# Adding the two halves of a compressed row by transfers and VectorE, and scoring all compressed keys of the prompt with the keys as the weights

## What is computed

```python
def compress(k, pe, wc):
    ...
    chunks = k[:, :n_chunk * CMP_STRIDE].reshape(bn, n_chunk, CMP_STRIDE, N_KV, HEAD_DIM)
    pe_r = pe.reshape(reps, CMP_STRIDE, 1, HEAD_DIM)
    w_r = wc.reshape(reps, CMP_STRIDE, HEAD_DIM, HEAD_DIM)
    return sum(jnp.einsum('bcsgh,she->bcge', chunks[:, r:r + n_cmp] + pe_r[r], w_r[r])
               for r in range(reps))

    # in the attention, for each query block
    s_c = jnp.einsum('bqgrh,bcgh->bqgrc', qg, kc) * scale
    p_c = masked_softmax(s_c, vis_c[None, :, None, None, :])
    o_c = jnp.einsum('bqgrc,bcgh->bqgrh', p_c.astype(vc.dtype), vc)
    ...
    o = g[..., 0:1] * o_c + g[..., 1:2] * o_s + g[..., 2:3] * o_w
```

## Time and profile before

| | |
|---|---|
| median of 3 runs | 821.28 us |
| the profiled execution | 820.7 us |
| its span in the trace | 819.1 us |
| TensorE matmul busy | 791.7 us (97%) |
| VectorE busy | 557.6 us (68%) |
| ScalarE busy | 392.7 us (48%) |
| mean granted TensorE clock | 0.993 |

### The profile page before, as it was taken

One profiled execution on the slowest core, in us unless ns is written; L12 is line 12 of the kernel. 1 busy time (PEld: TensorE's weight loads), 2 busy tenths in 40 slices (PEclk: granted clock), 3 DMA queues, 4 the chain that ended last, 5 costly groups with the idle time before them and its releaser, 6 DMA issues.

```text
span 819.1 us, 16906 instructions
## 1 busy us (share of the span) xinstructions
PE 791.7 (97%) x6364; PEld 731.9 (89%) x6364; DVE 557.6 (68%) x1044; ACT 392.7 (48%) x773; POOL 90.5 (11%) x165
## 2 busy tenths in 40 slices
PE   6999999999999999999789999999999999999994
PEld 6999598888889999999699987989888999999993
DVE  4676278887769675656567753698876886665664
ACT  4443236666365544443353422566655564444333
POOL 2330243000100000000023204410000000000000
PEclk9999999999999999999999999999999999999998
DMA  7877367542754655554357845665339456555531
GB/s 271 287 245 253 107 204 265 202 124 84 235 213 155 180 181 181 180 180 155 128 186 246 289 134 155 201 239 204 90 96 332 121 178 182 180 182 182 180 101 53
DMA packets 39482, 150.72 MB, mean 184 GB/s; under 512 B 5744, under 2 KB 5744, under 8 KB 38768
## 3 DMA queue, kind: packets, MB, share of 16 engines
q1 hardware_dynamic: 31104, 111.33, 42.0%
q0 software_dynamic: 8304, 38.37, 14.0%
HBM read 144.73 MB, written 13.34 MB: 193 GB/s over the span
## 4 chain that ended last, share of the span: by engine, by line
PE 92%; DVE 3%; ACT 3%; issue 1%; DMA 1%; SPq 0%; DVEq 0%; ACTq 0%
PE bank L594 22%; PE bank L595 22%; PE bank L596 22%; PE bank L678 3%; PE bank L798 3%; PE bank L628 1%; PE bank L642 1%; PE bank L748 1%; PE bank L605 1%; PE bank L754 1%; PE bank L839 1%; PE bank L919 1%; PE bank L680 1%; PE bank L778 1%; PE bank L728 1%
## 5 line engine op out<-in xcount | busy, mean ns | idle before, releaser
L594 PE MATMUL bank<-x_hi,w_hi 128*128 128x264 f32 x1200 | 351.6, 293 | 0.0
L596 PE MATMUL bank<-x_lo,w_hi 128*128 128x264 f32 x1200 | 341.1, 284 | 0.0
L595 PE MATMUL bank<-x_hi,w_lo 128*128 128x264 f32 x1200 | 340.8, 284 | 0.0
L1093 DVE TENSOR_TENSOR w_lo<-ring,w_hi 128x1024 fp32r<-128x1024 f32 x202 | 248.6, 1231 | 131.4 <-ACT w_hi L935 127.4
L935 ACT ACTIVATE w_hi<-ring 128x1024 fp32r<-128x1024 f32 x202 | 213.0, 1055 | 61.2 <-PE bank L596 34.3
L594 PEld LDWEIGHTS bank<-x_hi,w_hi 128*128 128x128 f32 x1200 | 226.8, 189 | 5.9 <-issue 4.9
L595 PEld LDWEIGHTS bank<-x_hi,w_lo 128*128 128x128 f32 x1200 | 227.0, 189 | 0.8
L596 PEld LDWEIGHTS bank<-x_lo,w_hi 128*128 128x128 f32 x1200 | 226.1, 188 | 0.0
L594 PE MATMUL bank<-h_rounded,w_hi 128*128 128x264 f32 x352 | 102.2, 290 | 0.0
L595 PE MATMUL bank<-h_rounded,w_lo 128*128 128x264 f32 x352 | 100.2, 285 | 0.0
L983 ACT ACTIVATE h<-bank 128x264 f32<-128x264 f32 x88 | 34.6, 393 | 121.2 <-PE bank L596 113.1
(11 more groups left out here) (239 smaller groups left out, 1002.6 us busy)
## 6 DMA issues: line engine op xcount, KB each, us to landing
ring<-weights_dram SPq DMA_DIRECT2D x206, 512.0 KB, 3.7
cache_a<-kcmp_dram POOLq DMA_DIRECT2D x32, 128.0 KB, 3.9
cache_b<-vcmp_dram POOLq DMA_DIRECT2D x32, 128.0 KB, 3.5
cache_a<-ksel_dram POOLq DMA_DIRECT2D x32, 128.0 KB, 2.7
cache_b<-vsel_dram POOLq DMA_DIRECT2D x32, 128.0 KB, 3.3
cache_a<-kwin_dram POOLq DMA_DIRECT2D x2, 2048.0 KB, 12.4
cache_b<-vwin_dram POOLq DMA_DIRECT2D x2, 2048.0 KB, 9.1
kv_dram<-h POOLq DMA_DIRECT2D x2, 1584.0 KB, 8.5
```

Of the source, the lines that this page charges most:

```text
L594: pe.matmul(out, w_high[:, k0 + k, :], high, start=(k == 0), stop=False)
L595: pe.matmul(out, w_rest[:, k0 + k, :], high, start=False, stop=False)
L596: ins = pe.matmul(out, w_high[:, k0 + k, :], rest, start=False, stop=(k == kn - 1))
L1093: dve.tensor_tensor(w_lo[:, slot % RING], ring[:, slot % RING], w_hi[:, d % HI_RING].bitcast(F32), ALU.subtract).then_inc(w_lo_ready, 1)
```

## The change

Three things are rewritten, and the order around them.

1. The halves of a compressed row are no longer added on TensorE. After the eviction SP copies each half of `halves` into the opposite partitions of a second buffer `other`, by two transfers of 64 x 640 elements for keys and two for values, on the queue of the weights. VectorE adds first half, second half and bias in one instruction for each of four blocks.
2. In `cmp_scores` the weights are now the 128 x 32 keys of `kc_bd`, four blocks of them beside each other in the array, and 256 query columns are the moving operand: 8 matmuls instead of 16. The scores come out transposed; ScalarE evicts them to `cs_t`, and a new step `cmp_back` turns them back by four transposes, from which VectorE goes on as before.
3. In the order, `cmp_vrows` moves behind `cmp_scores`, `cmp_soft` behind `dense 24`, and `cmp_turn` behind `dense 25`.

```diff
@@ -104,13 +104,11 @@
 order += [("cmp_k", 0), ("gates", 0), ("cmp_v", 0), ("cmp_sum", 0), ("cmp_sum", 1), ("dense", 21),
-          ("cmp_rope", 0), ("cmp_vrows", 0), ("dense", 22), ("cmp_scores", 0), ("dense", 23), ("cmp_soft", 0),
-          ("dense", 24)]
+          ("cmp_rope", 0), ("dense", 22), ("cmp_scores", 0), ("cmp_vrows", 0), ("dense", 23), ("cmp_back", 0),
+          ("dense", 24), ("cmp_soft", 0)]
     order.append(("scores", p))
-    if p == 0:
-        order.append(("cmp_turn", 0))
@@ -120,6 +118,8 @@
 nxt += 1
+if u == 0:
+    order.append(("cmp_turn", 0))
...
@@ -204,7 +202,7 @@
 "cmp_v": [OT, PT0], "cmp_rope": [MI],
-"cmp_vrows": [SB], "cmp_scores": [SA], "cmp_turn": [PT0], "one_cmp_scores": [SB],
+"cmp_vrows": [SB], "cmp_scores": [SA], "cmp_back": [PT1], "cmp_turn": [PT0], "one_cmp_scores": [SB],
@@ -249,8 +247,9 @@
 SPLIT_AT = plan_splits()
+CROSS_AFTER = {SLOT_CK: 0, SLOT_CV: 1}
 SLOTS_IN = [sum(1 for i in range(SLOTS) if i % RING == s) for s in range(RING)]
-VECTOR_STEPS = 101
+VECTOR_STEPS = 100
@@ -332,7 +331,9 @@
-halves = hf[:, 0:2 * 10 * 4 * CT].rearrange("p (v s g c) -> p v s g c", v=2, s=10, g=4)
+n_half = 2 * 10 * 4 * CT
+halves = hf[:, 0:n_half].rearrange("p (v s g c) -> p v s g c", v=2, s=10, g=4)
+other = hf[:, n_half:2 * n_half].rearrange("p (v s g c) -> p v s g c", v=2, s=10, g=4)
@@ -344,6 +345,7 @@
 cs = probs_flat[:, 768:768 + 32 * CT].rearrange("p (n c) -> p n c", c=CT)
+cs_t = probs_flat[:, 0:GP * SEQ]
...
@@ -438,6 +441,14 @@
+            def cross(l, which):
+
+                for j in range(2):
+                    wait_emptied(sp, l, ("cmp_k", "cmp_v")[which], 0, j)
+                for at in (0, HD):
+                    sp.dma_start(other[HD - at:2 * HD - at, which], halves[at:at + HD, which]
+                                 ).then_inc(other_landed[which], 16)
+
             load(slice(0, 1), 0)
@@ -454,6 +465,8 @@
 load(bass.ds(l * SLOTS + n, 1), i)
+if before in CROSS_AFTER and not following:
+    cross(l, CROSS_AFTER[before])
 if n == RING:
@@ -693,20 +706,9 @@
                         done(ins, step, i)
-                    elif step == "cmp_sum":
-
-                        out = out_bank(step, i)
-                        for j in range(2):
-                            wait_emptied(pe, l, "cmp_v" if i else "cmp_k", 0, j)
-                        for half in range(2):
-                            for g2 in range(2):
-                                ins = pe.matmul(out[g2 * HD:g2 * HD + HD, 0:10 * GP * NC].rearrange(
-                                    "p (s g c) -> p s g c", g=GP, c=NC), ident[:, half * HD:half * HD + HD],
-                                    halves[:, i, :, g2:4:2, half:half + NC], start=(half == 0), stop=(half == 1))
-                        done(ins, step, i)
                     elif step == "cmp_rope":
                         out = out_bank(step, i)
-                        wait_emptied(pe, l, "cmp_sum", 0)
+                        pe.wait_ge(kc_summed, l + 1)
                         done(pe.matmul(out[:, 0:288], perm, kc_all[:, :, :, :].rearrange("p g s c -> p (g s c)"),
@@ -722,12 +724,20 @@
     pe.wait_ge(roped, (l + 1) * len(ROPED))
+    for gp in range(GP):
+        for r in range(R):
+            ins = pe.matmul(out[32 * r:32 * r + 32, gp * SEQ:(gp + 1) * SEQ],
+                            kc_bd[:, gp, :, :].rearrange("p a b -> p (a b)"),
+                            h[:, Q + gp * R + r, 0:SEQ], start=(gp == 0), stop=(gp == GP - 1),
+                            skip_group_check=True)
+    done(ins, step, i)
+elif step == "cmp_back":
+    out = out_bank(step, i)
+    wait_emptied(pe, l, "cmp_scores", 0)
     for qi in range(2):
-        for n in range(8):
-            col = qi * 256 + n * 32
-            ins = pe.matmul(out[:, col:col + 32], h[:, Q + n, (1 - qi) * P:(2 - qi) * P],
-                            kc_bd[:, n // R, :, :].rearrange("p a b -> p (a b)"),
-                            start=True, stop=True)
+        for gp in range(GP):
+            col, src = qi * 256 + gp * P, gp * SEQ + (1 - qi) * P
+            ins = pe.transpose(out[:, col:col + P], cs_t[:, src:src + P], ident)
@@ -995,6 +1005,9 @@
         "p s g c -> p (s g c)"), bank[FILL[step, i, 1][0]][:, 0:CMP_OWN // KT8], ACT.Copy), step, i, 1)
+elif step == "cmp_scores":
+    wait_filled(act, l, step, i)
+    emptied_by(act.activation(cs_t, bank[SA][:, :], ACT.Copy), step, i)
@@ -1211,19 +1224,27 @@
 elif step == "cmp_sum":
-    which = i
-    b = FILL[step, i, 0][0]
-    wait_filled(dve, l, step, i)
-    link(dve.tensor_copy(bias[:, which:which + 1], bank[b][:, 18 * NC:18 * NC + 1]))
-    out = (vc_all if which else kc_all)[:, :, :, 0:NC].rearrange("p g s c -> p s g c")
-    src = bank[b][:, 0:18 * NC].rearrange("p (s g c) -> p s g c", g=GP, c=NC)
-    for gp in range(GP):
-        ins = dve.tensor_scalar(out[:, :, gp, :], src[:, :, gp, :], bias[:, which:which + 1], None,
-                                ALU.add)
-        if gp == 0:
-            link(ins)
-    emptied_by(ins, step, i)
-    if which:
+    dve.wait_ge(other_landed[i], (l + 1) * 2 * 16)
+    all_of = vc_all if i else kc_all
+    for g2 in range(2):
+        rows = slice(g2 * HD, g2 * HD + HD)
+        first, second = (other, halves) if g2 else (halves, other)
+        ins = dve.tensor_tensor(bias[rows, i:i + 1], first[rows, i, NB + 1, g2, 0:1],
+                                second[rows, i, NB + 1, g2, 1:2], ALU.add)
+    link(ins)
+    for g2 in range(2):
+        rows = slice(g2 * HD, g2 * HD + HD)
+        first, second = (other, halves) if g2 else (halves, other)
+        for gp in range(GP):
+            ins = dve.scalar_tensor_tensor(
+                out=all_of[rows, gp, 0:NB + 1, 0:NC], in0=first[rows, i, 0:NB + 1, 2 * gp + g2, 0:NC],
+                scalar=bias[rows, i:i + 1], in1=second[rows, i, 0:NB + 1, 2 * gp + g2, 1:CT],
+                op0=ALU.add, op1=ALU.add)
+    if i == 0:
+        ins.then_inc(kc_summed, 1)
+        dve.wait_ge(kc_summed, l + 1)
+    else:
+        link(ins)
@@ -1251,12 +1272,12 @@
                                bank[SB][:, 2 * P:4 * P]), step, i)
-elif step == "cmp_scores":
+elif step == "cmp_back":
     for qi in range(2):
-        ins = dve.tensor_tensor(cs[:, qi * 16:qi * 16 + 16, :], bank[SA][:, qi * 256:qi * 256 + 256]
+        ins = dve.tensor_tensor(cs[:, qi * 16:qi * 16 + 16, :], bank[PT1][:, qi * 256:qi * 256 + 256]
```

More of the change, by code:

```diff
@@ L196, in banks_of @@
         return [(PT0, PT1)[i]]
-    if step == "cmp_sum":
-        return [(PT1, SA)[i]]
     if step == "one_scores":
@@ L388, in trunk @@
         cmp_in_ready = sem("cmp_in_ready")
+        other_landed = [sem("other_k_halves_landed"), sem("other_v_halves_landed")]
         v_new_ready = sem("v_new_ready")
@@ L391, in trunk @@
         cmp_out_ready = sem("cmp_out_ready")
-        kc_ready = sem("kc_ready")
+        kc_ready, kc_summed = sem("kc_ready"), sem("kc_summed")
         cmp_shifted, cmp_exped, cmp_probs = sem("cmp_shifted"), sem("cmp_exped"), sem("cmp_probs")
```

## The result

The changed kernel is slower. Its median is 831.7 us (830.59 to 832.25, 4 runs), that of the kernel before, on the same chip, 821.71 us (820.14 to 822.3, 4 runs): 10 us more, a ratio of 1.0121 with a 95% interval of 1.0106 to 1.0136. The forecast was 822.0 us and its range ended at 825.6, so the measured time lies outside both. The profiled execution of the changed kernel took 832.25 us with a span of 830.6, against 820.7 and 819.1.

What follows compares the result with a forecast made beforehand. TensorE, busy 97% of the span, was taken as the bound. Its 4.44 us saving per layer met two waits: layer 1 +1.3, layer 2 -0.3, so 820.7 + 1.0 = 821.7, predicted as 822.0 us; range 818.6 to 825.6.

Steps and rivals of the forecast that it cites:

- TensorE issues 4.44 us less in a layer: TensorE's own work: 5.73 us of sums and scores gone, 1.29 of new scores and `cmp_back` added, in each layer.
- The values' transfers land at 104.6: First wait, layer 1: transfers issued about 100.9, queued behind the weight load, at the stores' pace, 0.3 us for page loads.
- the late bound of 105.8: Late end of the values' landing: 328 KB at the weight load's pace take 2.4 us after that load lands at 103.4.
- 103.0: Early end of the values' landing, from stores landing 2.1 us after issue; the early-landing rival had chance 0.10.
- VectorE needs 4.7 us from there to the keys: VectorE after the landing: sums, `vc_rep`, a weight's rest, rotation with `kc_bd`; keys ready at 109.3, TensorE waits 3.3 us.
- From the keys to `scores 0` 7.7 us, with the clock left at full: TensorE from 109.3 to 117.0: scores 0.9, `cmp_vrows` 0.39, a product 3.0, `cmp_back` 0.39, a product 3.0.
- The 1.5 us of layer 2, "taken as gone": Layer 2's loss at half clock behind the old compressed scores, 1.5 us, assumed to vanish with the change.
- The softmax chain is 2.4 us longer: Second wait: from `scores 0` to the second `turn` 17.66 us instead of 15.25, the compressed exponential coming behind `dense 24`'s eviction.
- the forecast's 134.7: Layer 1's restart in the second `turn`: 117.0 + 17.66, against 133.41 before, +1.3 us.
- The rival "values land late or the clock falls": Slower rival at TensorE's wait for `kc_ready`: late landing +1.2 in each layer, each clock fall +1.5; 824.4 to 828.5, chance 0.27.
- "A wait of 5 us (then 825 and more)": Sign that the forecast is wrong: TensorE waiting 5 us ahead of the compressed scores, where 2.5 to 4 was expected.
- a landing after 105.3 or one fall: Threshold for the slower rival: values landing after 105.3 in both layers, or one fall of the clock.

Runs made afterwards that it cites:

- the fillers: The changed kernel plus 48 extra matmuls with unused results, put right ahead of TensorE's wait for `kc_bd`; 826.47 us, ratio 1.0064.

## Why the prediction was wrong

Point by point, in layer 1, by its own steps:

- *TensorE issues 4.44 us less in a layer.* Right: it reached the wait at 106.01 (forecast 106.0), and with full clock the eight scores took 1.0 us (0.9).
- *The values' transfers land at 104.6.* **This step failed.** They were there at 107.1, 2.5 us later and beyond the late bound of 105.8. Two terms were mis-sized. GpSimd's pages, taken at 0.3 us by choice, cost 1.8 in these rows (some 1.3 by the means). And the pace was taken from four stores to DRAM: with the pages away it was still 4.73 us from first issue to use (4.35 in layer 2), where the forecast, without its 0.3 for the pages, had 3.7 (from 100.6, the first of its two issues, to 104.3). The issue, too, was taken at 0.33 us and takes 0.55. Each bound rested on one kind of transfer, and neither counted the other queue. In layer 2 it is 5.65 us from issue to use. The rule of the Trainium skill (DMA: Bandwidth & Descriptors, "Two DMAs through the same engine are not ordered") that was read as speaking against 103.0 pointed the right way: with the transfers in front of the load it was 2.3 us less from issue to use in layer 1, and 1.1 in layer 2.
- *VectorE needs 4.7 us from there to the keys.* 5.07 (107.12 to 112.19). The four sums took 1.27 us as four overlapping instructions (1.0), and the two tiny ones 0.32.
- *From the keys to `scores 0` 7.7 us, with the clock left at full.* **This step failed too**: 10.11, and 9.76 in layer 2. With the fillers it was 7.85 and 7.87, so 2.3 and 1.9 us are the clock's. The clock had a place among the rivals, at 1.5 us a fall; it fell in both layers, and for 6.8 us, where the stretch around had lasted 3.4. The 1.5 us of layer 2, "taken as gone", went the wrong way as well. That an idle TensorE loses its clock is also a rule of the Trainium skill (TensorE: Matmul & The Clock Gate, "Part 1: The HAM clock gate"); the run with the fillers agrees, with 2.3 us in layer 1. It isn't the only thing that goes before a fall here: the one at 513.9 in the kernel before came behind no wait.
- *The softmax chain is 2.4 us longer.* Right: 2.25 (17.50 against 15.25), with 1.86 at `scores 1` (forecast 1.8) and 1.22 at the second `turn` (1.5).

Layer 1: 2.5 + 0.4 + 2.4 - 0.2 = 5.1 us over the forecast's 134.7, which makes the 139.80. Layer 2: stage A is 4.2 us over the forecast (18.65 - 14.4), of which the longer wait (5.33 us against 3.3) has 2.0 and the clock most of the rest; the chain is as forecast (2.4 longer), and TensorE reaches `cmp_rope` 0.4 us earlier than forecast: 3.8. The fall at the last layer norm, which the runs tie to no part of the change, adds 1.7. Together 10.6 on 821.7 gives 832.3, against the profiled 832.25.

The rival "values land late or the clock falls" was what happened, with its place and mechanism as written; but its two parts were priced as mishaps that meet now and then (0.27, at most 828.5), where the first brought the second each time: in the four profiled kernels in which TensorE waited, with nothing to fill the time, 4.0 to 6.2 us behind the values, the clock fell in both layers. How long it stayed down did not follow the wait: 6.8 us in seven of the eight layers, and 3.4 behind 4.06 us in the eighth, while 4.04 us were followed by 6.8. "A wait of 5 us (then 825 and more)" was the sentence that fitted. The range was too narrow because its late end left out most of what the pages take of the DMA engines, and let the clock fall once. Its threshold was loose as well: a landing after 105.3 or one fall gives 823.1 or 823.2 by the forecast's own prices, not yet the 823.7 that it called slower.

## What to carry to other kernels

Work taken off the bounding engine pays only if nothing it waits for stands behind the new path: here the same instructions gave 831.7 or 814.98 us by the place of two steps in the order, so put the step that waits for a transfer behind the one the bounding engine needs, before judging the transfer. Bound the landing of a new transfer by everything that is on the DMA engines in that window, the loads of the same queue and those of other queues, not by a quiet one. And price a new wait of TensorE with the half clock behind it: here 6.2 us of idle time cost 8.4 (6.18 + 2.26). A shorter wait did not surely bring that second part down: behind 4.4 us it was 2.8 (10.61 - 7.85), behind 4.1 us 1.5. Last, before a stretch of half clock is charged to a change, look where the time is lost: the same 3.4 us at half clock cost 0.1 us in front of a wait that it merely used up, and 1.7 at the last layer norm, where nothing came behind to take it up.

## What the runs showed of the hardware

- Two transfers from SBUF to SBUF of 64 partitions by 640 float32 (160 KB each), issued together: 4.2 to 4.6 us from the first issue to first use beside 128 KB page loads with no load in front, 4.4 to 4.8 behind a 512 KB load without pages, 5.6 to 6.5 behind it and beside them. SP takes 0.55 us to issue each, against 0.34 for the 512 KB load.
- Behind idle times of TensorE of 4.0 to 6.2 us the granted clock was 0.50 for 3.4 or 6.8 us in every profiled kernel that had one, in both layers, and stayed at 1.00 in both layers where matmuls filled the same time. Behind waits of 1.8 to 1.9 us it fell in 4 of 14 layers, behind one of 1.53 us in 6 of 22. At 0.50 a product's matmuls start 0.22 us apart instead of 0.12.
- `bank<-h,kc_bd` with 32 weight columns, four of them beside each other: 16 instructions of 256 columns in 1.0 us at full clock.
- Four additions of 64 x 135 with a bias take 1.27 us on VectorE, 0.32 each.
